# Two DiT layers on one core: the gate's modulation columns move into the down-projection, and VectorE takes half of the transpose copies

## The chip, the cores and the metric

The kernel runs on one core of one Trainium2 chip. The metric is the device time of one execution in microseconds; lower is better. Three executions of the kernel before were timed.

## The reference, cut to what matters

Two layers run over 640 tokens of width 1024: 128 context tokens and 512 latent tokens. Each layer computes

```python
sh1, sc1, ga1, sh2, sc2, ga2 = split(silu(cond) @ ada_w + ada_b, 6)   # 6 x 1024 values, for 2 conditions
h = rmsnorm(x, g_pre_mix) * (1 + sc1) + sh1
mixed = mixer(h @ w_in)              # 8 retention heads, 8 neighbourhood-attention heads
x = x + ga1 * rmsnorm(mixed @ w_out, g_post_mix)
h = rmsnorm(x, g_pre_ffn) * (1 + sc2) + sh2
x = x + ga2 * rmsnorm(conv_ffn(h, w_up, conv_w, conv_b, w_down), g_post_ffn)
```

The two conditions are one vector for the context tokens and one for the latent tokens. `ga2`, the gate of the feed-forward part, is not needed before the end of `w_down`'s product. Inside the neighbourhood attention a softmax over 320 to 384 keys is followed by a product with the values.

## The kernel before, in words

Everything is written out by hand: five engine programs (SP issues transfers, ACT, DVE, PE, POOL), each a fixed order of instructions, tied by counting semaphores. Every matmul in fp32 is made of three products of a high and a low part, so each operand is split: ACT copies the high part (`w_hi`, `m_hi`, `aT_hi`), DVE subtracts it to get the low part (`w_lo`, `m_lo`, `aT_lo`).

**The stream.** All weights come through one ring of four slots, `raw`, 128 x 1024 values (512 KB) each. `SP` loads the items of a layer in one fixed order (L541 to L548), item s into slot s % 4, and waits with each until the item four places ahead in that slot has been freed. A weight item is freed by its `split_lo` on DVE (L1350). A *column item* (128 of the 6144 modulation values, against all 1024 inputs) is not used by PE at all: DVE multiplies and sums it against each of the two conditions, `ada_first` (L1360) and `ada_second` (L1368), into `mod`; the second one frees the slot. The order of the items is `ORDER` (L97) up to the output projection (w is a weight, a is a column), then the up-projection, then `stream_down` and `stream_ada`.

**The columns.** 48 per layer. 0 to 15 (`sh1`, `sc1`) are computed one layer ahead, in the down-projection; 16 to 23 are `ga1`, 24 to 39 `sh2` and `sc2`, 40 to 47 `ga2`. Before, 19 of the columns 16 to 47 are done in the input projection and retention, 8 in the attention loop, 5 in the second half of the output projection. `times_gain` (L1378) then multiplies in a norm weight, and ACT stores a finished gate to DRAM (`store_gates`) and loads it again broadcast to all partitions (`gb_mix`, `gb_ffn`). `mod_done` counts the finished groups.

**The attention loop** runs over 20 pairs of a head group and a block of queries, in a software pipeline of NPU + 3 = 23 rounds. In round i PE computes the scores of pair i (L2369, L2371), the transposes of pair i - 1 (L2380, two heads e = 0 and 1, banks 4 and 5) and the product with the values of pair i - 2 (L2393). DVE adds the bias and takes the maximum (`na_weigh`, L1600), ACT does the exponentials (L1158) and copies the transposes of both heads from PSUM to `pt` (L1166). Every fourth round there is also the division by the sums (L1889, L1891, L2404, L1895). In round 1 to 5 DVE also has `mix_low` (L1582) and in round 5 `split_lo(31)`; in rounds 5 to 20 it has one half of a column each (L1365 or L1371).

**The down-projection** has 24 granules (two halves of 12). A granule is one weight item with one or two blocks of 128 rows of `w_down`, against the matching blocks `kt` of the activations `m`: 30 matmuls, or 15 where there is one block (granules 10, 11, 12 and 13). In its iteration `gi` ACT runs `split_hi` of weight gi + 2 and then `down_high` for the blocks of granule gi; DVE runs one column (where there is one), `split_lo` of weight gi + 2, and then `down_low` for the blocks of granule gi. The blocks 4 and 5 (granule 2) are the exception on DVE: their `down_low` stands ahead of the loop, while their `down_high` is in ACT's iteration 2, behind `split_hi` of weight 4. The first items of a half are, before: w0 w1 w2 w3 a w4 a w5 a w6 and so on, that is, weight 4 is the sixth item and lies in slot 1, and weight 5 is the eighth, in slot 3.

Of the kernel before, what the change touches and what calls it, by code (L numbers as in the profile page):

```python
# [64 lines left out]
ADA_MIX = 5 * KD  # L65
# [22 lines left out]
S_UP0 = G_IN + G_OUT + ADA - ADA_FIRST  # L88
S_DOWN0 = S_UP0 + G_UP
S_HALF = (G_DOWN + ADA_FIRST) // 2  # L90
# [9 lines left out]
assert len(W_POS) == G_IN + G_OUT and len(A_POS) == ADA - ADA_FIRST  # L100
# [12 lines left out]
def stream_down(q):  # L113

    n, i = divmod(q, G_HALF)
    return S_DOWN0 + S_HALF * n + (i if i < 4 else 2 * i - 3)


def stream_ada(col):

    if col < ADA_FIRST:
        n, i = divmod(col, ADA_FIRST // 2)
        return S_DOWN0 + S_HALF * n + 4 + 2 * i
    return A_POS[col - ADA_FIRST]
# [43 lines left out]
def build(nc, t):  # L168
    with ExitStack() as ctx:
# [154 lines left out]
        mod_done = counted("mod_done", 5, 0, 6)  # L324
# [50 lines left out]
        na_p = counted("na_p", 2 * NPU)  # L375
# [4 lines left out]
        gates_out = counted("gates_out", 16 * 4)  # L380
# [213 lines left out]
        MOD_PRE, MOD_ALL = 2, 5  # L594
# [170 lines left out]
        def _(act):  # L765
# [29 lines left out]
            def modulate(w, tt, layer):  # L795
# [4 lines left out]
                if tt == 0:  # L800
                    act.wait_ge(mod_done, at(mod_done, layer, MOD_ALL if w else MOD_PRE))
                    if w:
                        act.wait_ge(pad_done, at(pad_done, layer, 1))
# [112 lines left out]
            def store_gates(w, layer):  # L916

                for c in range(2):
                    act.dma_start(gates[layer, w, c].rearrange("(k p) -> p k", p=P),
                                  mod[:, (3 * w + 2) * KD:(3 * w + 3) * KD, c],  # L920
                                  allow_slow_non_contiguous=True).then_inc(gates_out, 16)

            def load_gates(w, gb, layer):

                act.wait_ge(gates_out, at(gates_out, layer, 32 * (w + 1)))
                act.dma_start(gb[:].rearrange("p c d -> p (c d)"),
                              gates[layer:layer + 1, w].rearrange("o c d -> o (c d)").to_broadcast([P, 2 * D])
                              ).then_inc(gates_in, 16)

# [160 lines left out]
            for layer in range(DEPTH):  # L1090
# [77 lines left out]
                for i in range(NPU + 3):  # L1168
                    for e in range(2):
                        if i < NPU:  # L1170
                            exponentials(i, e)
                        if 1 <= i < NPU + 1:
                            copy_transposed(i - 1, e)
# [6 lines left out]
                    if i == 18:  # L1180
                        act.wait_ge(mod_done, at(mod_done, layer, MOD_ALL - 1))
                        store_gates(0, layer)
# [11 lines left out]
                load_gates(0, gb_mix, layer)  # L1194
# [11 lines left out]
                def load_ffn_gates(n):  # L1206
                    for c in range(2):
# [141 lines left out]
        def _(dve):  # L1349
# [10 lines left out]
            def ada_first(col, layer):  # L1360
                s = stream_ada(col)
                dve.wait_ge(*full(s, layer))
                n = col - ADA_FIRST if col >= ADA_FIRST else col + ADA - ADA_FIRST
                dve.wait_ge(ada_part, at(ada_part, layer, n))
                dve.tensor_tensor_reduce((ada_junk if col < ADA_FIRST else ada_sq)[:], raw[:, s % 4, :], cond[:, 0, :], 1.0, ada_start(col, layer), ALU.mult,  # L1365
# [12 lines left out]
            def times_gain(f0, c0, plus, layer):  # L1378
# [1413 lines left out]
```

## Time and profile before

| | |
|---|---|
| runs | 1604.45, 1601.09, 1603.74 us; median 1603.74 us |
| span of the profiled execution | 1601.0 us |
| PE busy | 1575.8 us (98%) |
| DVE busy | 1275.6 us (80%) |
| ACT busy | 794.1 us (50%) |
| chain that ended last | PE 84%, DVE 7%, issue 2%, ACT 2%, DMA 1% |

The span runs from the first to the last instruction; a time of its own for the profiled execution is not given beside it, and the span lies 2.7 us under the median of the runs. "Busy" of PE is modelled from pipelined matmuls, so 98% is not peak speed. An idle time in brackets behind an instruction names what it waited for last.

### The profile page before, as it was taken

Reading aid. Unit: us, or ns where it says so; the run is one execution under the profiler, and the core shown is the slowest. Engines: PE = TensorE matmul, PEld = TensorE weight load, DVE = VectorE, ACT = ScalarE, POOL = GpSimd, SP = SyncE. Lnnn points to the kernel's source line nnn. Section 1 sums busy time; section 2 is a strip of 40 time slices with the busy share of each in tenths; the row PEclk is TensorE's granted clock in tenths of the full one; section 3 lists DMA queues with packets and bytes.
Section 4 is the critical chain, followed back from the end, with each engine's and each line's share of the span. In section 5 each row is a group of like instructions: output and inputs, shape, how many; then the busy total and the mean of one; then the engine's idle time right before and its main releaser. Section 6 shows DMA issues by size and latency. Waiting matters only on the chain.

```text
span 1601.0 us, 28310 instructions
## 1 busy us (share of the span) xinstructions
PE 1575.8 (98%) x9688; PEld 1389.2 (87%) x9688; DVE 1275.6 (80%) x2255; ACT 794.1 (50%) x1483; POOL 379.2 (24%) x302
## 2 busy tenths in 40 slices
PE   8999999999999999999999999999999999999998
PEld 6788898689999999888878889967899999998886
DVE  7876677968999999966669556987689999998575
ACT  5433235638655565533383323274766565563333
POOL 0031033001455455200000400700035455541000
PEclk9999999999999999999999999999999999999999
DMA  9343265361222222454414414736312222335451
GB/s 369 122 132 111 74 222 179 95 168 55 66 81 89 79 92 79 148 168 158 152 40 145 138 54 134 260 107 146 79 64 82 80 91 79 92 92 178 125 184 66
DMA packets 65494, 195.04 MB, mean 122 GB/s; under 512 B 15361, under 2 KB 16769, under 8 KB 65153
## 3 DMA queue, kind: packets, MB, share of 16 engines
q1 hardware_dynamic: 50114, 175.54, 35.1%
q10 hardware_dynamic: 15296, 18.39, 3.5%
q8 instruction: 53, 0.87, 0.3%
q14 instruction: 31, 0.25, 0.1%
HBM read 187.05 MB, written 6.85 MB: 121 GB/s over the span
## 4 chain that ended last, share of the span: by engine, by line
PE 84%; DVE 7%; issue 2%; ACT 2%; DMA 1%; ACTq 1%; DVEq 0%; SPq 0%
PE bank L2087 14%; PE bank L2088 13%; PE bank L2089 13%; PE bank L2597 10%; PE bank L2599 10%; PE bank L2598 10%; DMA raw<-in_stream 1%; PE bank L2393 1%; PE bank L2457 1%; PE bank L2455 1%; PE bank L2453 1%; PE bank L2380 1%; PE bank L2109 1%; DVE w_lo L1354 1%; PE bank L2277 1%
## 5 line engine op out<-in xcount | busy, mean ns | idle before, releaser
L778 ACT ACTIVATE w_hi<-raw 128x1024 fp32r<-128x1024 f32 (+1 forms) x120 | 123.1, 1029 | 389.0 <-PE bank L2089 325.1
L1354 DVE TENSOR_TENSOR w_lo<-raw,w_hi 128x1024 fp32r<-128x1024 f32 (+1 forms) x128 | 156.3, 1228 | 162.4 <-ACT w_hi L778 162.2
L2087 PE MATMUL bank<-w_hi,aT_lo 128*128 128x512 f32 x520 | 210.5, 405 | 2.1 <-DVE aT_lo L1787 2.0
L2088 PE MATMUL bank<-w_lo,aT_hi 128*128 128x512 f32 x520 | 206.0, 396 | 0.0
L2089 PE MATMUL bank<-w_hi,aT_hi 128*128 128x512 f32 x520 | 205.6, 395 | 0.0
L2597 PE MATMUL bank<-aT_hi,w_lo 128*128 128x322 f32 x640 | 199.8, 312 | 4.5 <-DVE u L1953 4.5
L2598 PE MATMUL bank<-aT_lo,w_hi 128*128 128x322 f32 x640 | 199.4, 312 | 0.0
L2599 PE MATMUL bank<-aT_hi,w_hi 128*128 128x322 f32 x640 | 198.6, 310 | 0.0
L1252 ACT ACTIVATE w_hi<-raw 128x512 fp32r<-128x512 f32 x200 | 117.8, 627 | 105.8 <-POOL raw L660 105.8
L2087 PE MATMUL bank<-w_hi,m_lo 128*128 128x512 f32 x400 | 158.5, 396 | 0.0
L2088 PE MATMUL bank<-w_lo,m_hi 128*128 128x512 f32 x400 | 157.3, 393 | 0.0
L2089 PE MATMUL bank<-w_hi,m_hi 128*128 128x512 f32 x400 | 157.2, 393 | 0.0
L1942 DVE TENSOR_TENSOR w_lo<-raw,w_hi 128x512 fp32r<-128x512 f32 x200 | 140.7, 734 | 0.0
L2597 PEld LDWEIGHTS bank<-aT_hi,w_lo 128*128 128x128 f32 x640 | 120.7, 189 | 6.0 <-DVE u L1953 5.0
L2598 PEld LDWEIGHTS bank<-aT_lo,w_hi 128*128 128x128 f32 x640 | 121.3, 190 | 0.0
L2599 PEld LDWEIGHTS bank<-aT_hi,w_hi 128*128 128x128 f32 x640 | 121.3, 190 | 0.0
L2087 PEld LDWEIGHTS bank<-w_hi,aT_lo 128*128 128x128 f32 x520 | 98.2, 189 | 26.5 <-DVE aT_lo L1787 3.4
L2089 PEld LDWEIGHTS bank<-w_hi,aT_hi 128*128 128x128 f32 x520 | 98.4, 189 | 23.3
L2088 PEld LDWEIGHTS bank<-w_lo,aT_hi 128*128 128x128 f32 x520 | 98.4, 189 | 20.8
L649 POOL TENSOR_TENSOR raw<-raw 128x512 f32<-128x512 f32 x40 | 52.6, 1316 | 258.6 <-DVE bank L1983 137.4
L639 POOL TENSOR_TENSOR bias<-bias,masks 128x192 f32<-128x192 f32 (+1 forms) x48 | 59.1, 1269 | 198.0 <-DMA bias<-in_bias 198.0
L2599 PE MATMUL bank<-s_hi,w_hi 128*128 128x322 f32 x320 | 99.8, 312 | 0.0
(287 smaller groups left out, 3865.9 us busy)
## 6 DMA issues: line engine op xcount, KB each, us to landing
raw<-in_stream SPq DMA_DIRECT2D x304, 512.0 KB, 3.6
lead<-in_lead SPq DMA_DIRECT2D x16, 512.0 KB, 10.6
bias<-in_bias ACTq DMA_DIRECT2D x8, 896.0 KB, 10.3
na_v<-vn ACTq DMA_DIRECT2D x2, 1280.0 KB, 5.6
x<-in_xs SPq DMA_DIRECT2D x4, 512.0 KB, 12.4
vt<-na_v ACTq DMA_DIRECT2D x16, 128.0 KB
gb_mix<-gates ACTq DMA_DIRECT2D x2, 1024.0 KB, 6.2
gb_ffn<-gates ACTq DMA_DIRECT2D x8, 256.0 KB, 4.5
```

Of the source, the lines that this page charges most:

```text
L639: i_ = pool.tensor_tensor(part, part, masks[:, m0 * CG:(m0 + n) * CG].rearrange("p (g c) -> p g c", c=CG).unsqueeze(2) .to_broadcast([P, n ...
L649: pool.tensor_tensor(g_, g_, a_, ALU.subtract).then_inc(t1_done, 1)
L778: act.activation(w_hi[:, g % 4, 0:n], raw[:, s % 4, 0:n], ACT.Copy).then_inc(hi_done, 1)
L1252: act.activation(block_of(w_hi, n), block_source(n, e), ACT.Copy).then_inc(blk_hi, 1)
L1354: dve.tensor_tensor(w_lo[:, g % 4, 0:n], raw[:, s % 4, 0:n], w_hi[:, g % 4, 0:n].bitcast(F32), ALU.subtract).then_inc(raw_free[s % 4], 1)
L1942: i_ = dve.tensor_tensor(block_of(w_lo, n), block_source(n, e), block_of(w_hi, n).bitcast(F32), ALU.subtract)
L2087: pe.matmul(out, ll, rh, start=start, stop=False)
L2088: pe.matmul(out, lh, rl, start=False, stop=False)
L2089: return pe.matmul(out, lh, rh, start=False, stop=stop)
L2597: pe.matmul(out, wl, rhs_hi[:, k, :], start=k == 0, stop=False)
L2598: pe.matmul(out, wh, rhs_lo[:, k, :], start=False, stop=False)
L2599: i_ = pe.matmul(out, wh, rhs_hi[:, k, :], start=False, stop=k == HP - 1)
```

## The change

1. Columns 40 to 47 (`ga2`) leave the attention's place in the stream; the eight a's between w31 and w32 are gone from `ORDER`. DVE's attention loop has no column any more (columns 35 to 39 now fill the five places in the output projection).
2. They go to the down-projection of the same layer, four in each half, ahead of the next layer's eight of that half. So a half has 12 columns in place of 8. They are spread over the iterations i = 4 to 11 of a half as 2, 1, 2, 1, 2, 1, 2, 1. The items of a half are now w0 w1 w2 w3 a a w4 a w5 a a w6 a w7 and so on: weight 4 is the seventh item (slot 2), weight 5 the ninth (slot 0).
3. DVE copies the transposes of the second head (e = 1), ACT only those of the first. PE waits on a semaphore of each.
4. The gate's store is split in two and moves from the output projection into ACT's iterations gi = 7 and 19 (before `down_high`), the loads to gi = 9 and 21; before they stood ahead of the loop (just before `down_weight(3)`) and at gi = 14.
5. `times_gain` for `sh2`/`sc2` and `ga2` are moved with their columns, so `mod_done` counts 6.

```diff
-ORDER = ("wwww" "wwww" "waawaaww" "wwaawwaa" "wwww" "wwawawaaa" "wwaawaawwaawww" "aaaaaaaa" "waawaawaw")
+ORDER = ("wwww" "wwww" "waawaaww" "wwaawwaa" "wwww" "wwawawaaa" "wwaawaawwaawww" "waawaawaw")
...
 def stream_down(q):
     n, i = divmod(q, G_HALF)
-    return S_DOWN0 + S_HALF * n + (i if i < 4 else 2 * i - 3)
+    return S_DOWN0 + S_HALF * n + (i if i < 4 else i + down_columns(i + 1))
+
+def down_columns(i):
+    return 0 if i < 4 else (3 * (i - 4) + 1) // 2
...
                 for i in range(NPU + 3):
-                    for e in range(2):
-                        if i < NPU:
-                            exponentials(i, e)
-                        if 1 <= i < NPU + 1:
-                            copy_transposed(i - 1, e)
+                    if i < NPU:
+                        exponentials(i, 0)
+                    if 1 <= i < NPU + 1:
+                        copy_transposed(i - 1, 0)
+                    if i < NPU:
+                        exponentials(i, 1)
...
-                act.wait_ge(mod_done, at(mod_done, layer, MOD_ALL))
-                store_gates(1, layer)
                 turn_ffn(layer)
-                act.wait_ge(gates_out, at(gates_out, layer, 64))
...
-                load_ffn_gates(0)
                 down_weight(3)
...
-                    if gi == G_HALF + 2:
-                        act.wait_ge(y_copied, at(y_copied, layer, 2 * NT))
-                        load_ffn_gates(1)
+                    if i == 7:
+                        store_ffn_gates(n, layer)
+                    if i == 9:
+                        if n:
+                            act.wait_ge(y_copied, at(y_copied, layer, 2 * NT))
+                        load_ffn_gates(n)
...
+            def copy_transposed(u, layer):
+                n = P * len(spans_of(PAIRS[u]))
+                dve.wait_ge(na_t, at(na_t, layer, 2 * u + 2))
+                if u >= 2:
+                    dve.wait_ge(na_av, at(na_av, layer, u - 1))
+                dve.tensor_copy(pt[:, u % 2, 1, 0:n], bank[NA_T[1]][:, 0:n]).then_inc(na_q, 1)
...
-                    if 5 <= i < 21:
-                        (ada_first if i % 2 else ada_second)(ADA_FIRST + 19 + (i - 5) // 2, layer)
+                    if 1 <= i < NPU + 1:
+                        copy_transposed(i - 1, layer)
...
                         n, i = divmod(gi + 2, G_HALF)
-                        if i >= 4:
-                            ada(ADA_FIRST // 2 * n + i - 4, layer)
+                        for col in ADA_DOWN[n][down_columns(i):down_columns(i + 1)]:
+                            ada(col, layer)
+                        if i == 7:
+                            dve.wait_ge(*freed(stream_ada(ADA_DOWN[n][HALF_K - 1]), layer))
+                            times_gain(ADA_LATE + HALF_K * n, C_PF + HALF_K * n, 0.0, layer, HALF_K).then_inc(mod_done, 1)
                         split_lo(W_DOWN0 + gi + 2, layer)
```

What the instructions look like in order, at three places. First DVE at the start of the down-projection, from the `down_low` of blocks 4 and 5 to that of blocks 6 and 7, before (L1365 and L1371 are the two parts of a column, L1354 is `split_lo`, L1987 `down_low`; the `ISA mod` rows read out a sum):

```order
L1987 TENSOR_TENSOR m_lo<-m,m_hi 128x642 x2
L1365 ISA ada_junk,mod<-raw,cond 128x1024
L1365 ISA mod 128x1
L1371 ISA raw,mod<-raw,cond 128x1024
L1371 ISA mod 128x1
L1354 TENSOR_TENSOR w_lo<-raw,w_hi 128x1024
L1365 ISA ada_junk,mod<-raw,cond 128x1024
```

and the same place in the changed kernel (L2008, L1380, L1386 and L1370 are the same lines there):

```order
L2008 TENSOR_TENSOR m_lo<-m,m_hi 128x642 x2
L1380 ISA ada_junk,mod<-raw,cond,par 128x1024
L1380 ISA mod 128x1
L1386 ISA raw,mod<-raw,cond,par 128x1024
L1386 ISA mod 128x1
L1380 ISA ada_junk,mod<-raw,cond,par 128x1024
L1380 ISA mod 128x1
L1386 ISA raw,mod<-raw,cond,par 128x1024
L1386 ISA mod 128x1
L1370 TENSOR_TENSOR w_lo<-raw,w_hi 128x1024
```

A second column stands ahead of `split_lo` of weight 4; the columns are now those of the gate, which start from `par`. Second, ACT at the same place, before: `down_weight(3)`, the SiLU, then `split_hi` of weight 4 and `down_high` of blocks 4 and 5.

```order
L1229 ACTIVATE cvg<-bank,par 128x322
L1230 ACTIVATE cvg<-bank,par 128x320
L1208 DMA gb_ffn<-gates 128x512 x2
L1267 ACTIVATE w_hi<-raw 128x1024
L1213 ACTIVATE cvg<-cvg 128x642
L778 ACTIVATE w_hi<-raw 128x1024
L1261 ACTIVATE m_hi<-m 128x642 x2
```

and now:

```order
L1243 ACTIVATE cvg<-bank,par 128x322
L1244 ACTIVATE cvg<-bank,par 128x320
L1281 ACTIVATE w_hi<-raw 128x1024
L1227 ACTIVATE cvg<-cvg 128x642
L788 ACTIVATE w_hi<-raw 128x1024
L1275 ACTIVATE m_hi<-m 128x642 x2
```

Only the two loads of `gb_ffn` have gone from here; `m_hi` still stands behind the split of weight 4. Third, DVE in the attention's rounds 5 and 6, before:

```order
L1354 TENSOR_TENSOR w_lo<-raw,w_hi 128x1024
L1365 ISA ada_sq,mod<-raw,cond,par 128x1024
L1365 ISA mod 128x1
L1889 RECIPROCAL rec<-esum 128x8
L1891 COPY nao<-bank 128x512
L1600 ISA sp,nmax<-bank,bias 128x384
L1600 ISA nmax 128x1
L1371 ISA raw,mod<-raw,cond,par 128x1024
L1371 ISA mod 128x1
L1895 TENSOR_TENSOR nao<-nao,bank 128x512
```

and now:

```order
L1370 TENSOR_TENSOR w_lo<-raw,w_hi 128x1024
L1623 COPY pt<-bank 128x384
L1910 RECIPROCAL rec<-esum 128x8
L1912 COPY nao<-bank 128x512
L1615 ISA sp,nmax<-bank,bias 128x384
L1615 ISA nmax 128x1
L1623 COPY pt<-bank 128x384
L1916 TENSOR_TENSOR nao<-nao,bank 128x512
```

In each round a half column has given way to a copy of 128 x 384.

## Rows read from the trace of the kernel before

**Rows 1.** Page, part 4: the chain that ended last, by engine.
```profile
PE 84%; DVE 7%; issue 2%; ACT 2%; DMA 1%; ACTq 1%; DVEq 0%; SPq 0%
```
**Rows 2.** By stretch: length; PE, PEld, DVE, ACT, POOL busy; clock, DMA share, GB/s.
```profile
262.00:284.00 22.00, 19.74 (x192) 13.77 (x191) 14.19 (x38) 17.48 (x48) 0.00 (x0) 1.00 0.30 98
284.00:320.00 36.00, 35.25 (x357) 25.03 (x357) 34.38 (x91) 26.23 (x87) 0.00 (x0) 1.00 0.36 91
665.00:680.00 15.00, 15.00 (x66) 11.95 (x65) 15.00 (x19) 5.06 (x7) 4.33 (x1) 1.00 0.55 175
```
**Rows 3.** Timeline of the attention, rounds 6 to 20: start us, us, instruction, [idle before <-releaser].
```profile
282.10 1.09 PE L2404 MATMUL bank<-ident,rec 128*64 128x128 f32 x16 [0.41 <-DVE nao L1891]
282.91 1.28 DVE L1371 CUSTOM_DVE_ANT_0 raw<-raw,cond,par 128x1024 f32<-128x1024 f32 x1
284.72 0.48 DVE L1600 CUSTOM_DVE_ANT_0 sp<-bank,bias 128x320 f32<-128x320 f32 x1
284.75 0.52 PE L2380 MATMUL bank<-ident,sp 128*128 128x128 f32 x3 [0.33 <-ACT pt L1166]
...
286.76 1.21 PE L2380 MATMUL bank<-ident,sp 128*128 128x128 f32 x6
...
295.61 0.87 PE L2380 MATMUL bank<-ident,sp 128*128 128x128 f32 x6
...
319.04 0.45 ACT L1166 ACTIVATE pt<-bank 128x128 f32<-128x128 f32 x2 [1.55 <-PE bank L2380]
```
**Rows 4.** Groups by line and form, ACT and DVE: busy us, mean ns.
```profile
L1166 ACT ACTIVATE pt<-bank 128x384 f32<-128x384 f32 x64 | 30.3, 474 | 0.0
L1891 DVE COPY nao<-bank 128x512 f32<-128x512 f32 x10 | 6.5, 649 | 1.4 <-PE bank L2393 1.4
```
**Rows 5.** Timeline of DVE at the start of the down-projection; last row: layer 1.
```profile
668.31 2.94 DVE L1987 TENSOR_TENSOR m_lo<-m,m_hi 128x642 fp32r<-128x642 f32 x2
671.16 1.22 DVE L1365 CUSTOM_DVE_ANT_0 ada_junk<-raw,cond 128x1024 f32<-128x1024 f32 x1
...
673.45 1.22 DVE L1354 TENSOR_TENSOR w_lo<-raw,w_hi 128x1024 fp32r<-128x1024 f32 x1
...
678.02 1.55 DVE L1987 TENSOR_TENSOR m_lo<-m,m_hi 128x642 fp32r<-128x642 f32 x2
...
1450.04 2.94 DVE L1987 TENSOR_TENSOR m_lo<-m,m_hi 128x642 fp32r<-128x642 f32 x2
```
**Rows 6.** Timeline of ACT and of SP's issues at the same place.
```profile
659.04 0.33 SPq L548 DMA_DIRECT2D raw<-in_stream  x1
666.49 1.06 ACT L778 ACTIVATE w_hi<-raw 128x1024 fp32r<-128x1024 f32 x1 [1.07 <-PE bank L2089]
667.41 0.33 SPq L548 DMA_DIRECT2D raw<-in_stream  x1
667.46 1.35 ACT L1261 ACTIVATE m_hi<-m 128x642 fp32r<-128x642 f32 x2
668.54 0.33 SPq L548 DMA_DIRECT2D raw<-in_stream  x1
673.63 1.06 ACT L778 ACTIVATE w_hi<-raw 128x1024 fp32r<-128x1024 f32 x1 [4.82 <-PE bank L2089]
680.58 1.06 ACT L778 ACTIVATE w_hi<-raw 128x1024 fp32r<-128x1024 f32 x1 [4.62 <-PE bank L2089]
```
**Rows 7.** Transfers: issue to landing, `raw` in 655 to 700 us; the gates' stores.
```profile
DMA to landing us min/median/max: 3.4/3.6/4.6
...
gates<-mod ACTq DMA_DIRECT2D x4, 4.0 KB, 11.1
```
**Rows 8.** Timeline of ACT and DVE at the start of the second half.
```profile
739.59 1.22 DVE L1365 CUSTOM_DVE_ANT_0 ada_junk<-raw,cond 128x1024 f32<-128x1024 f32 x1
...
747.19 1.56 DVE L1987 TENSOR_TENSOR m_lo<-m,m_hi 128x642 fp32r<-128x642 f32 x2
...
750.22 1.06 ACT L778 ACTIVATE w_hi<-raw 128x1024 fp32r<-128x1024 f32 x1 [2.95 <-PE bank L2089]
```

More of the change, by code:

```diff
@@ L115, in stream_down @@
     n, i = divmod(q, G_HALF)
-    return S_DOWN0 + S_HALF * n + (i if i < 4 else 2 * i - 3)
+    return S_DOWN0 + S_HALF * n + (i if i < 4 else i + down_columns(i + 1))
+def down_columns(i):
+    return 0 if i < 4 else (3 * (i - 4) + 1) // 2
 def stream_ada(col):
-    if col < ADA_FIRST:
-        n, i = divmod(col, ADA_FIRST // 2)
-        return S_DOWN0 + S_HALF * n + 4 + 2 * i
+    for n in range(2):
+        if col in ADA_DOWN[n]:
+            a = ADA_DOWN[n].index(col)
+            return S_DOWN0 + S_HALF * n + a + next(i for i in range(4, G_HALF) if down_columns(i + 1) > a)
     return A_POS[col - ADA_FIRST]
@@ L800, in modulate @@
                 if tt == 0:
-                    act.wait_ge(mod_done, at(mod_done, layer, MOD_ALL if w else MOD_PRE))
+                    act.wait_ge(mod_done, at(mod_done, layer, MOD_FFN if w else MOD_PRE))
                     if w:
@@ L1362, in ada_first @@
                 dve.wait_ge(*full(s, layer))
-                n = col - ADA_FIRST if col >= ADA_FIRST else col + ADA - ADA_FIRST
-                dve.wait_ge(ada_part, at(ada_part, layer, n))
-                dve.tensor_tensor_reduce((ada_junk if col < ADA_FIRST else ada_sq)[:], raw[:, s % 4, :], cond[:, 0, :], 1.0, ada_start(col, layer), ALU.mult,
+                dve.wait_ge(ada_part, at(ada_part, layer, ADA_ORDER.index(col)))
+                dve.tensor_tensor_reduce((ada_sq if ADA_FIRST <= col < ADA_LATE else ada_junk)[:], raw[:, s % 4, :], cond[:, 0, :], 1.0, ada_start(col, layer), ALU.mult,
                                          ALU.add, mod[:, col, 0:1]).then_inc(ada_part, 1)
@@ L1376, in ada, with times_gain @@
                 ada_second(col, layer)
-            def times_gain(f0, c0, plus, layer):
+            def times_gain(f0, c0, plus, layer, n=KD):
                 c0 += layer * NPAR
-                return dve.scalar_tensor_tensor(mod[:, f0:f0 + KD, :], mod[:, f0:f0 + KD, :], plus,
-                                                par[:, c0:c0 + KD].unsqueeze(2).to_broadcast([P, KD, 2]),
+                return dve.scalar_tensor_tensor(mod[:, f0:f0 + n, :], mod[:, f0:f0 + n, :], plus,
+                                                par[:, c0:c0 + n].unsqueeze(2).to_broadcast([P, n, 2]),
                                                 ALU.add, ALU.mult)
@@ L1392, in modulate @@
                 dve.wait_ge(norm_tp, at(norm_tp, layer, i + 1))
-                dve.wait_ge(mod_done, at(mod_done, layer, MOD_ALL if w else MOD_PRE))
+                dve.wait_ge(mod_done, at(mod_done, layer, MOD_FFN if w else MOD_PRE))
                 for k in range(KV):
@@ L1879, in _ @@
                         split_lo(31, layer)
-                    if 5 <= i < 21:
-                        (ada_first if i % 2 else ada_second)(ADA_FIRST + 19 + (i - 5) // 2, layer)
+                    if 1 <= i < NPU + 1:
+                        copy_transposed(i - 1, layer)
                     if i == 14:
-                        dve.wait_ge(*freed(stream_ada(ADA_MIX - 1), layer))
-                        times_gain(4 * KD, C_GF, 1.0, layer).then_inc(mod_done, 1)
+                        dve.wait_ge(*freed(stream_ada(3 * KD - 1), layer))
                         times_gain(2 * KD, C_PM, 0.0, layer).then_inc(mod_done, 1)
@@ L1910, in _ @@
                     split_lo(W_OUT0 + 4 + g, layer)
-                    for col in range(ADA_MIX + 3 + 2 * g, ADA_MIX + 3 + 2 * g + n):
+                    for col in range(ADA_FIRST + 19 + 2 * g, ADA_FIRST + 19 + 2 * g + n):
                         ada(col, layer)
-                dve.wait_ge(*freed(stream_ada(ADA - 1), layer))
-                times_gain(5 * KD, C_PF, 0.0, layer).then_inc(mod_done, 1)
+                dve.wait_ge(*freed(stream_ada(ADA_LATE - 1), layer))
+                times_gain(4 * KD, C_GF, 1.0, layer).then_inc(mod_done, 1)
                 split_lo(W_OUT0 + 7, layer)
@@ L2377, in na_transposes @@
                     if u >= 1:
-                        pe.wait_ge(na_p, at(na_p, layer, 2 * u - 1 + e))
+                        copied = na_q if e else na_p
+                        pe.wait_ge(copied, at(copied, layer, u))
                     for i, (c0, p0, n, tile) in enumerate(spans_of(PAIRS[u])):
@@ L2384, in na_values @@
                 g, jb = PAIRS[u]
-                pe.wait_ge(na_p, at(na_p, layer, 2 * u + 2))
+                pe.wait_ge(na_p, at(na_p, layer, u + 1))
+                pe.wait_ge(na_q, at(na_q, layer, u + 1))
                 if jb == 0 and g >= 2:
```

46 lines of the change are left out of this document (27 added, 19 removed).

## The prediction, made before the changed kernel was run

> **What bounds the kernel.** I read the page's chain of waits first. PE carries 84% of it and DVE only 7% [rows 1], so an instruction taken from DVE or ACT is worth something only at the few places where PE stands behind them, and one added costs nothing until PE has to wait for it. So I read the two stretches that the change touches. In the attention loop PE is busy for 19.74 of 22 us and 35.25 of 36 us [rows 2]: it idles for 2.26 + 0.75 = 3.0 us per layer, most of it in the first third. That is all that lighter ACT and DVE programs can win there, 6 us in both layers. At the start of the down-projection PE is busy for all of 15 us, and so is DVE [rows 2]: there is no slack to be seen on DVE just where the change adds work. The prediction is decided there.
>
> **Attention: what the change saves.** It removes 16 half columns per layer from DVE (1.28 us in [rows 3]) and adds 20 copies of 128 x 384 out of PSUM. The trace has no such copy on DVE: a copy of 128 x 512 takes 649 ns there, and one of 128 x 384 takes 474 ns on ACT [rows 4]. Three quarters of the first are 0.49 us, and some of an instruction doesn't shrink with its size, so I take 0.52 us; the ends change nothing on PE. ACT loses 20 copies of 0.47 us [rows 4]. DVE is 16 x 1.28 - 20 x 0.52 = 10 us lighter per layer, but only PE's waits count.
> - Rounds 6 and 7. The half column at 282.91 holds the weighing back to 284.72, although its scores are there earlier; PE's transposes then idle for 0.33 us, and the next six take 1.21 us where six without a wait take 0.87 [rows 3]. Without the columns the weighing starts 0.8 us earlier, behind the division only. I take back the 0.33 and 0.34 us and 0.2 us that the loading of the weights hides: 0.9 us.
> - The last rounds. Both copies of pair 19 wait for PE's transposes and run one behind the other on ACT (0.45 us together), with PE behind them [rows 3]; in parallel they take half: 0.25 us. Small waits of PE elsewhere: 0.15 us.
> - No gain in rounds 2 to 4, where PE waits for `mix_low`, which keeps its place. No gain at PE's 0.41 us before 282.10 [rows 3] either: the copy of pair 4 now stands behind `mix_low` and `split_lo(31)` on DVE and comes about 0.5 us later than ACT's did. The second head's transposes start that much later and use up what the earlier copy of `nao` gives.
>
> Sum: 0.9 + 0.25 + 0.15 = 1.3 us per layer. It can't be more than 3.0 [rows 2]; if the late copy in round 5 is not absorbed, it is a loss of 0.5 with nothing against it.
>
> **Output projection and its turn: nothing.** DVE has five columns there as before and one `times_gain` either way. ACT loses two store issues that stood behind finished work; PE is never idle there, and it covers this.
>
> **Down-projection: the added work.** DVE takes 2.29 us for a column (671.16 to 673.45, [rows 5]), 1.14 us for a `split_lo`, and 1.48 us for two `down_low`. Two iterations cost 3 x 2.29 + 2 x 2.62 = 12.1 us, against two granules of PE of 6.95 us each (673.63 to 680.58, [rows 6]) = 13.9 us. So in the steady part DVE keeps up. At the start it doesn't.
>
> *Weight 4 comes late.* Before, it goes to slot 1 and is issued at 659.04. Now the two columns go first, and it gets slot 2, whose issue is the one at 667.41 [rows 6], when DVE has done `split_lo` of weight 2. A load lands after 3.6 us [rows 7]: 671.0. ACT splits it from 671.1 (now 666.49) and only then makes `m_hi` of blocks 4 and 5, from 672.05 to 673.4 (now from 667.46). DVE has their `down_low` ahead of everything else, so it stands idle from 668.3 with two columns ready in `raw`, and ends at 674.3 in place of 671.16 [rows 5]. PE wants these blocks when granule 1 ends, at 673.5 [rows 6]: it starts at 674.4, **0.9 us** late.
>
> *Then two columns stand in front.* DVE: 674.3 + 4.58 (two columns) + 1.14 + 2.29 + 1.14 + 1.48 = 684.95 for blocks 6 and 7, which now are ready at 679.5, 1.0 us before granule 3 [rows 5, 6]. PE wants them at 674.4 + 6.95 = 681.35: **3.7 us** late, with 0.1 us of signalling. Weight 5 (slot 0, freed by the first column at 676.6) lands at 680.4 and its split and the blocks' `m_hi` are done by 682.8: hidden.
>
> *Granule 4*: 684.95 + 4.58 + 1.14 + 1.48 = 692.15, wanted at 685.05 + 6.95 = 692.0: **0.2 us** with the signal. Then DVE gains 1.8 us in every two granules, and nothing is late.
>
> *Second half.* Granules 12 and 13 take half the time, so DVE has to catch up again: from 739.59 [rows 8] it needs 4.58 + 1.14 + 2.29 + 1.14 + 1.48 = 10.65, until 750.25; now it is done with blocks 0 and 1 at 748.7. Granule 14 ends at about 750.1 [rows 8]: **0.2 us**, and the next double column costs **0.2 us** more (757.45 against 757.3).
>
> Sum: 0.9 + 3.7 + 0.2 + 0.4 = 5.2 us per layer. Layer 1 has the same schedule 781.7 us later [rows 5]: 10.4 us. A load that takes 3.4 or 4.6 us [rows 7] changes the first term by -0.2 or +1.0 per layer. The other bound is that DVE starts unhindered by weight 4, with the double columns alone; that is the second rival.
>
> The Trainium skill ("DMA: Bandwidth & Descriptors", section on the anatomy of one DMA) gives about 2.0 us plus the bytes over 436 GB/s, which is 3.2 us for such a load, fitted on loads that GpSimd issues. By that estimate weight 4 would be 0.4 us earlier than by the row, and the sum 0.8 us lower; I go by the row, since it is of this very load at this place.
>
> **The gate's transfers.** A store takes 11.1 us to land [rows 7]. ACT now waits for it two granules (13.9 us) after its issue: 2.8 us of room, so nothing. The four issues stand before `down_high` in iterations where ACT is idle for over 4 us per granule (4.62 us in [rows 6]). The loads at gi = 9 and 21 have two granules before they are used. The two loads that leave ACT at the start lay beside idle time.
>
> **Sum against the runs.** 10.4 - 2.6 = +7.8 us. The sum is made on an execution with a span of 1601.0 us, 2.7 us below the runs' median; it is a difference, and I add it to the median: 1603.7 + 7.8 = **1611.5 us**. A measurement of this kernel can tell about 0.2% (3.2 us) from no change.
>
> **The rivals.**
> - *Slower as worked out* (DVE is late at the start of the down-projection, and weight 4's slot is why): 1611.5 us, between 1606.5 (gain of 2.5 and stalls of 4 us per layer) and 1616. Chance 0.66.
> - *No change: only the second column counts.* If weight 4's place in the ring costs nothing, blocks 6 and 7 are ready at 679.5 + 2.29 = 681.8, wanted at 680.5: 1.4 us, with the second half's 0.4 us 1.8 per layer. 3.6 - 2.6 = +1.0: 1604.7 us. For it: the columns' transfers themselves come early. Against it: ACT is a fixed order, and `m_hi` of blocks 4 and 5 stands behind the split of weight 4. Chance 0.12.
> - *Faster: the attention decides.* All of PE's 3.0 us per layer come back, since both engines it waits for are lighter, and the stalls stay under that. With the 1.8 us of the last rival: 3.6 - 6.0 = -2.4; with none -6.0, 1597.7 us. The point is a stall of 1.3 us per layer by my gain, 3.0 by the largest. For it: DVE is busy for 34.38 of 36 us there [rows 2]. Against it: most of PE's idle time is in the early rounds, at `mix_low`, which stays. Chance 0.07.
> - *Slower by more: DVE doesn't recover.* The ring's items now free each other in a closer sequence (weight 6 waits for the column of iteration 3, weight 7 for a column of iteration 4), and small stores go on beside it. With loads of 4.6 us, or 1 us lost at every second granule, 4 to 8 us are added: 1616 to 1620 us. Against it: DVE's 1.8 us per two granules. Chance 0.15.
>
> **Range and chances.** 1611.5 is the likeliest. The range goes from 1604.5, which takes in the second case, to 1617.5, the lower part of the last. Slower by over 0.2%: 0.66 + 0.15 = 0.81. Within 0.2%: 0.12. Faster: 0.07.
>
> **What would show it.** In the changed profile the attention should be some 1.3 us shorter, with no column in it and PE's second wait of 0.33 us gone. The SP issue after 667 should be weight 4's; ACT's first split in the loop should wait for a transfer and begin near 671 less the attention's gain; DVE should idle for some 4 us before the `down_low` of blocks 4 and 5. PE should show waits for `m_lo` of about 0.9 and 3.7 us in the first three granules of each layer, and two small ones in the second half. The prediction is wrong if ACT's `m_hi` of blocks 4 and 5 is on time, if PE has no idle time at the start of the down-projection, or if PE waits at every second granule.

## The result and the profile after

| | before | changed |
|---|---|---|
| median of the runs | 1603.64 us (4 runs, 1601.09 to 1604.45) | 1629.55 us (4 runs, 1627.23 to 1630.42) |
| span of the profiled execution | 1601.0 us | 1625.4 us |
| attention, from PE's first transposes to its last, either layer | 55.23 us | 53.43 us |
| down-projection, start of granule 0 to the last matmul that reads the low part of `m`, layers 0 and 1 | 153.59 and 152.66 us | 169.39 and 166.16 us |

The changed kernel is slower: ratio 1.0162, 95% interval 1.0150 to 1.0174. I had forecast 1611.5 us and a range up to 1617.5. The sign was right and the size was not: +25.9 us in place of +7.8. In the two stretches of the table it gains 3.6 us and loses 29.3 us; the difference is 25.7 us. The two spans differ by 24.4 us only, because the profiled execution of the kernel before has one stretch at half clock in the up-projection of layer 1, for 1.4 us, which the changed one doesn't have (last section).

The page of the changed kernel, parts 1 and 4 (rows that answer to [rows 1]):

```profile
PE 1582.1 (97%) x9688; PEld 1392.6 (86%) x9688; DVE 1290.9 (79%) x2297; ACT 782.4 (48%) x1443; POOL 378.2 (23%) x302
...
PE 74%; DVE 12%; issue 4%; DMA 3%; ACT 2%; ACTq 1%; DVEq 0%; SPq 0%
```

PE's share of the chain falls by ten points; DVE, the issues and DMA take them. That DMA is among them is the first sign of something the prediction had not costed. The waits of PE, changed kernel; columns: us in total, times, longest:

```profile
PE bank L2111 <- DVE m_lo L2008: 18.2, 8, 4.4
```

This row has no counterpart before: 18.2 us of new waits, all for `down_low` (waits under 0.15 us are not in it). Where they lie shows in the starts of the granules (the first matmul of each in PE's timeline; a granule takes 6.95 us when nothing is late):

| layer 0 | before | changed | longer by |
|---|---|---|---|
| granules 0 to 3 | 659.30 to 687.29 | 656.62 to 692.09 | 7.48 us |
| 4 to 13 | to 742.98 | to 747.89 | 0.11 us |
| 14 to 16 | to 763.88 | to 770.13 | 1.34 us |
| 17, 18 | to 777.80 | to 784.05 | 0.00 us |
| 19 to 21 | to 798.66 | to 811.78 | 6.87 us |

In layer 1 the same groups are 7.56, 0.04, 1.31, 0.00 and 4.60 us longer. So there are three places per layer; the first two were forecast, the third was not. First the start. ACT, changed kernel (answers to [rows 6]):

```profile
668.28 1.06 ACT L788 ACTIVATE w_hi<-raw 128x1024 fp32r<-128x1024 f32 x1 [5.55 <-DMA raw<-in_stream]
669.25 1.35 ACT L1275 ACTIVATE m_hi<-m 128x642 fp32r<-128x642 f32 x2
677.73 1.06 ACT L788 ACTIVATE w_hi<-raw 128x1024 fp32r<-128x1024 f32 x1 [7.13 <-DMA raw<-in_stream]
```

DVE, changed kernel (answers to [rows 5]):

```profile
670.07 1.56 DVE L2008 TENSOR_TENSOR m_lo<-m,m_hi 128x642 fp32r<-128x642 f32 x2 [4.38 <-ACT m_hi L1275]
...
681.06 1.56 DVE L2008 TENSOR_TENSOR m_lo<-m,m_hi 128x642 fp32r<-128x642 f32 x2
```

That is the mechanism as forecast: the split of weight 4 waits for its transfer, `m_hi` stands behind it, DVE idles for 4.38 us, and then two columns stand in front of blocks 6 and 7, and the one of weight 5. These are columns of the gate, which start from `par`: DVE takes 2.41 us for each (671.56 to 673.97), where the sum had 2.29. PE's first matmul of granule 3:

```profile
682.77 0.76 PE L2111 MATMUL bank<-w_hi,m_lo 128*128 128x512 f32 x1 [3.80 <-DVE m_lo L2008]
```

Granule 3 itself then takes 9.32 us in place of 6.95. The stretches around it and around granule 20; columns as in [rows 2], the clock third from the end:

```profile
679.00:682.00 3.00, 0.00 (x0) 0.00 (x0) 3.00 (x5) 1.04 (x2) 0.00 (x0) 0.82 0.78 300
682.00:685.00 3.00, 2.23 (x5) 1.82 (x6) 3.00 (x6) 0.00 (x0) 0.00 (x0) 0.50 0.75 251
685.00:688.00 3.00, 3.00 (x9) 2.34 (x8) 3.00 (x7) 2.31 (x3) 0.00 (x0) 0.54 0.61 187
688.00:691.00 3.00, 3.00 (x15) 2.42 (x14) 3.00 (x6) 0.00 (x0) 0.00 (x0) 1.00 0.86 238
...
795.00:800.00 5.00, 4.46 (x11) 3.52 (x12) 5.00 (x8) 2.35 (x3) 0.00 (x0) 0.50 0.96 370
```

The same stretch of the kernel before, for comparison:

```profile
685.00:688.00 3.00, 3.00 (x15) 2.41 (x14) 1.76 (x4) 0.45 (x1) 0.00 (x0) 1.00 0.54 190
```

PE is idle for all of 679 to 682, and behind it the granted clock stands at 0.50, the 1.2 GHz level, where the kernel before has 1.00: 9 matmuls in 3 us in place of 15. This second price of a wait was in no term of the prediction.

The third place. ACT, changed kernel, around the gate's second store:

```profile
777.36 0.98 ACTq L929 DMA_DIRECT2D gates<-mod  x2
778.44 1.37 ACT L1275 ACTIVATE m_hi<-m 128x642 fp32r<-128x642 f32 x2
791.61 1.06 ACT L788 ACTIVATE w_hi<-raw 128x1024 fp32r<-128x1024 f32 x1 [11.80 <-DMA raw<-in_stream]
```

The transfers of 774 to 800 us, changed kernel (count, KB each, median us to landing):

```profile
raw<-in_stream SPq DMA_DIRECT2D x8, 512.0 KB, 9.0
...
gates<-mod ACTq DMA_DIRECT2D x2, 2.0 KB, 14.2
```

Beside the store the median load of the stream takes 9.0 us, against 3.6 in [rows 7], and 12.6 us in the same place of layer 1 (1568 to 1592 us). I had asked only when the store itself would land. The trace of the kernel before would have told the rest. Its transfers of 346 to 361 us, around the store in the output projection:

```profile
raw<-in_stream SPq DMA_DIRECT2D x1, 512.0 KB, 12.8
gates<-mod ACTq DMA_DIRECT2D x2, 4.0 KB, 12.3
```

There nobody was waiting for that load; in the down-projection somebody is.

### The profile page after: what moved, and what is told of

Read it like the earlier page. It is cut to its first block, busy times and chain, and to the rows that moved or that the text cites. A ratio compares the mean times of both kernels' runs of the same rounds, so it can differ in the third digit from the quotient of the medians.

```text
span 1625.4 us, 28346 instructions
## 1 busy us (share of the span) xinstructions
PE 1582.1 (97%) x9688; PEld 1392.6 (86%) x9688; DVE 1290.9 (79%) x2297; ACT 782.4 (48%) x1443; POOL 378.2 (23%) x302
## 4 chain that ended last, share of the span: by engine, by line
PE 74%; DVE 12%; issue 4%; DMA 3%; ACT 2%; ACTq 1%; DVEq 0%; SPq 0%
PE bank L2111 11%; PE bank L2112 10%; PE bank L2113 10%; PE bank L2623 9%; PE bank L2625 9%; PE bank L2624 9%; DMA raw<-in_stream 3%; DVE ada_junk L1380 2%; PE bank L2419 2%; DVE w_lo L1370 2%; DVE m_lo L2008 1%; PE bank L2405 1%; PE bank L2483 1%; PE bank L2481 1%; PE bank L2479 1%
## 5 line engine op out<-in xcount | busy, mean ns | idle before, releaser
L1370 DVE TENSOR_TENSOR w_lo<-raw,w_hi 128x1024 fp32r<-128x1024 f32 (+1 forms) x128 | 156.5, 1230 | 141.5 <-ACT w_hi L788 141.2
L2111 PE MATMUL bank<-w_hi,m_lo 128*128 128x512 f32 x400 | 162.8, 407 | 18.5 <-DVE m_lo L2008 18.2
L2112 PE MATMUL bank<-w_lo,m_hi 128*128 128x512 f32 x400 | 160.8, 402 | 0.0
L2111 PEld LDWEIGHTS bank<-w_hi,m_lo 128*128 128x128 f32 x400 | 77.3, 193 | 41.0 <-issue 23.3
```

The source lines that it names most:

```text
L1370: dve.tensor_tensor(w_lo[:, g % 4, 0:n], raw[:, s % 4, 0:n], w_hi[:, g % 4, 0:n].bitcast(F32), ALU.subtract).then_inc(raw_free[s % 4], 1)
L2111: pe.matmul(out, ll, rh, start=start, stop=False)
L2112: pe.matmul(out, lh, rl, start=False, stop=False)
```

## The experiments

Ten kernels, each beside runs of the kernel before on the same chip (medians 1603.19 to 1603.55 us). Two theories were left after the profile: that the early columns and the store are two separate causes (A in most expectations), and rivals that put all on one of them or on something else. "Changed" means the changed kernel.

### a_late: the columns later

```diff
 def down_columns(i):
-    return 0 if i < 4 else (3 * (i - 4) + 1) // 2
+    return 0 if i < 4 else i - 4 if i < 8 else 4 + 2 * (i - 8)
```

> Changed kernel, but the 12 columns of a half are spread as 1, 1, 1, 1, 2, 2, 2, 2 over the iterations 4 to 11 in place of 2, 1, 2, 1, 2, 1, 2, 1, so the first items of a half stand in the ring as in the kernel before. Theory A (the start of each half is what the double column costs): no wait before granules 2, 3 and 15, no halved clock in granule 3; saves 7.5 + 1.2 us per layer, 17 us in all: about 1612 us, if the last four iterations (4.58 + 2.62 = 7.2 us of DVE against 6.95 of PE) stay hidden. Theory B (what counts is the ring's pace beside the gate's store, which now falls among the double columns): the wait before granule 20 or 21 grows to 7 us or more and a wait shows behind the store of the first half too: 1617 to 1623 us.

Measured: 1624.30 us, ratio 1.0125 [1.0108, 1.0142], above the numbers of both theories. Each had half of it. Granules 2, 3 and 15 show no wait and keep the kernel before's pace (granule 4 starts 27.98 us after granule 0, before 27.99). But waits stand behind the stores now: 3.77 and 4.50 us in layer 0, 6.63 and 4.62 us in layer 1, before granules 8 and 20. ACT's splits behind the store of gi = 7, layer 0:

```profile
714.98 0.63 ACT L788 ACTIVATE w_hi<-raw 128x512 fp32r<-128x512 f32 x1 [12.15 <-DMA raw<-in_stream]
715.51 1.35 ACT L1275 ACTIVATE m_hi<-m 128x642 fp32r<-128x642 f32 x2
718.77 0.63 ACT L788 ACTIVATE w_hi<-raw 128x512 fp32r<-128x512 f32 x1 [1.91 <-DMA raw<-in_stream]
```

In the changed kernel the store of gi = 7 had cost PE nothing. With two columns per granule beside it, it does. That fits a price that depends on how many items the ring must bring while the store lasts. It isn't the whole of it: in the changed kernel the stores of gi = 7 and 19 have the same three columns per two granules beside them. The loads beside the first took up to 11.2 us and PE waited for none; beside the second they took up to 16.3 us and PE waited. Why the second is the slower is not settled.

### a_nostore: without the gate's stores

```diff
-                store_gates(1, HALF_K * n, HALF_K * (n + 1), layer)
```

(and the loads of `gb_ffn` read the mixer's gate, with no wait on the stores)

> Changed kernel without the four stores of the feed-forward gate per layer (left out: the feed-forward gate's values; the loads of the gate bring the mixer's gate instead, so the output is another). Theory A (the small pieces of the stores slow the loads of the stream): loads of the stream at 774 to 800 us take some 3.6 to 4.6 us again, the waits of 4.39 and 2.98 us before granule 20 and the clock that they cost go; saves 6.9 and about 5 us: 1618 us. Theory B (DVE's 12 columns or, in layer 0, the loads of the next layer's inputs do it): the wait of layer 0 stays over 2 us, and the time above 1624 us.

Measured: 1616.68 us, ratio 1.0082 [1.0065, 1.0099]: theory A's number within 1.4 us. This kernel leaves the feed-forward gate's values out. Granules 17 to 23 keep their pace in both layers. The waits at the start stay as they were (1.07 and 3.78 us in layer 0). In 774 to 800 us, where the next layer's loads run in layer 0:

```profile
raw<-in_stream SPq DMA_DIRECT2D x7, 512.0 KB, 5.4
```

So those loads alone bring the median to 5.4 us, without a wait of PE; the store brings it to 9.0. In layer 1, where no next layer is loaded, the median without the store is 3.6 us, with it 12.6.

### b_stores: the stores moved in the kernel before

```diff
-                store_gates(1, layer)
                 turn_ffn(layer)
...
-                    if gi == G_HALF + 2:
-                        act.wait_ge(y_copied, at(y_copied, layer, 2 * NT))
-                        load_ffn_gates(1)
+                    if i == 7:
+                        store_gates(1, KD // 2 * n, KD // 2 * (n + 1), layer)
+                    if i == 9:
+                        if n:
+                            act.wait_ge(y_copied, at(y_copied, layer, 2 * NT))
+                        load_ffn_gates(n)
```

> Kernel before, with the feed-forward gate's store cut in two and moved to gi = 7 and 19 and the loads to gi = 9 and 21, as the change does; the columns stay. Theory A (the stores cost only because the ring has 2.5 items per granule in place of 2): loads of the stream beside the stores take 7 to 10 us here as well, but PE waits less than 1 us for them: 1603 to 1606 us. Theory B (the stores stall the stream by themselves): a wait of over 2 us before granule 20 or 21 and a halved clock, 1610 us or more.

Measured: 1603.28 us, ratio 1.0003 [0.9994, 1.0013], and no wait for `m_lo` in the down-projection. Yet its transfers of 774 to 800 us are slow too:

```profile
raw<-in_stream SPq DMA_DIRECT2D x6, 512.0 KB, 7.8
```

The same stores at the same place cost nothing with 2 items per granule and, in the changed kernel, 11.5 us with 2.5.

### a_row6: the same store in rows

PE transposes the four finished columns of each condition (128 x 4 into 4 x 128) ahead of granules 6 and 18, ACT copies them out of PSUM, and 8 rows of 512 bytes are stored per half in place of 1024 pieces of 4 bytes.

```diff
+                        if i == 6:
+                            pe.wait_ge(mod_done, at(mod_done, layer, MOD_LATE + n))
+                            if n:
+                                pe.wait_ge(gt_cp, at(gt_cp, layer, 1))
+                            k0 = 5 * KD + HALF_K * n
+                            for c in range(2):
+                                i_ = pe.transpose(bank[7][0:HALF_K, c * P:(c + 1) * P], mod[:, k0:k0 + HALF_K, c], ident[:])
+                            i_.then_inc(gt_tp, 1)
...
-                store_gates(1, HALF_K * n, HALF_K * (n + 1), layer)
+                act.activation(ada_sq[0:HALF_K, 0:2 * P], bank[7][0:HALF_K, 0:2 * P], ACT.Copy).then_inc(gt_cp, 1)
+                act.wait_ge(gt_cp, at(gt_cp, layer, n + 1))
+                for c in range(2):
+                    act.dma_start(gates[layer, 1, c, HALF_K * n * P:HALF_K * (n + 1) * P].rearrange("(k p) -> k p", p=P),
+                                  ada_sq[0:HALF_K, c * P:(c + 1) * P]).then_inc(gates_out, 16)
```

> Changed kernel with its columns as they are (2, 1, 2, 1 and so on) and only the gate's store in rows, with PE's transposes ahead of granule 6. Theory A (the number of small pieces is what delays the loads, not the place of the store): the waits before granule 20 go as in a_nostore, those before granules 2, 3 and 15 stay: 1616 to 1618 us. Theory B (a store of any form costs): a wait of over 1 us stays before granule 20, 1621 us or more.

Measured: 1617.30 us, ratio 1.0082 [1.0067, 1.0098], the ratio of a_nostore. The same bytes leave at the same place, and the wait before granule 20 is gone; those before granules 2, 3 and 15 stay. The loads of 774 to 800 us are as without a store (5.4 us there), and those of layer 1 take 3.6 us again:

```profile
raw<-in_stream SPq DMA_DIRECT2D x8, 512.0 KB, 5.1
```

It is the small pieces, not the store, that held up the loads.

### a_w4first: weight 4 ahead of its columns

```diff
-    return S_DOWN0 + S_HALF * n + (i if i < 4 else i + down_columns(i + 1))
+    return S_DOWN0 + S_HALF * n + (i if i <= 4 else i + down_columns(i + 1))
...
+                        if i == 4:
+                            split_lo(W_DOWN0 + gi + 2, layer)
                         for col in ADA_DOWN[n][down_columns(i):down_columns(i + 1)]:
                             ada(col, layer)
```

> Changed kernel, but weight 4 of each half lies ahead of its two columns in the ring, and DVE splits it ahead of them. Theory A (weight 4's late load and the doubled column are two separate costs, and a wait of PE of some 4 us takes the clock with it): PE's wait of 0.99 us before granule 2 goes, that of 3.8 us before granule 3 falls to about 1.4 us (the price of one more column of 2.29 us against 1.0 us of room), and the 2.4 us that granule 3 lost to the halved clock come back. Saves 1.0 + 2.4 + 2.4 = 5.8 us per layer, 11.5 us in all: 1618 us. Theory B (it is the columns alone, wherever weight 4 lies): the wait before granule 3 stays above 3 us and the time within 3 us of 1629.5.

Measured: 1628.64 us, ratio 1.0151 [1.0134, 1.0168]: theory B's time, though not for its reason. The start did improve: no wait before granule 2, one of 1.91 us in place of 3.80 before granule 3. But that one halves the clock as well (granule 3 takes 8.58 us), the wait before granule 15 grows from 0.68 to 2.26 us, and that before granule 20 from 4.39 to 6.17 us. ACT and DVE at the start, and DVE in the second half:

```profile
676.00 1.06 ACT L788 ACTIVATE w_hi<-raw 128x1024 fp32r<-128x1024 f32 x1 [7.62 <-DMA raw<-in_stream]
676.96 1.35 ACT L1275 ACTIVATE m_hi<-m 128x642 fp32r<-128x642 f32 x2
...
679.10 1.21 DVE L1370 TENSOR_TENSOR w_lo<-raw,w_hi 128x1024 fp32r<-128x1024 f32 x1
680.24 1.55 DVE L2008 TENSOR_TENSOR m_lo<-m,m_hi 128x642 fp32r<-128x642 f32 x2
...
744.49 1.23 DVE L1370 TENSOR_TENSOR w_lo<-raw,w_hi 128x1024 fp32r<-128x1024 f32 x1 [1.50 <-ACT w_hi L788]
```

ACT waits for the transfer of weight 5, but that is not what holds PE: its split ends at 677.0 and DVE, busy without a gap from 664 to 691 us, takes it up at 679.10. What is left of the wait is work of DVE: three columns of 2.41 us in a row in place of two of 2.29, 2.65 us more, against 0.8 us of room (679.5 to 680.3 in the kernel before). That is more than the 1.4 us expected, and enough to halve the clock. In the second half DVE now has to wait 1.50 us for ACT's split of weight 4 before it can begin the two columns, where the changed kernel began them at once: so the wait before granule 15 grows. The start gains 3.8 us per layer (granules 0 to 3), the second half loses 1.6 and 1.3 us, and granules 19 to 21 lose 1.6 and 3.8 us. The last needn't be the edit's: in a_actcopy (below), with the order of the changed kernel, the waits before granule 20 are 5.69 and 3.62 us in place of 4.39 and 2.98.

### b_wait4 and b_wait8: what a wait of PE costs

The kernel before, with four or eight dummy subtractions on DVE ahead of the `down_low` of blocks 6 and 7.

```diff
+                        if gi == 3 and kt == 6:
+                            for j in range(4):
+                                if j:
+                                    dve.wait_ge(delay, at(delay, layer, j))
+                                dve.tensor_tensor(bank[7][:], cond[:, 0, 0:W], cond[:, 1, 0:W], ALU.subtract).then_inc(delay, 1)
```

> Kernel before, with four dummy subtractions of 128 x 512 values (about 0.68 us each, 2.7 us) on DVE ahead of the down_low of blocks 6 and 7, in both layers: those blocks were ready 1.0 us before PE wanted them, so PE waits about 1.8 us before granule 3, with the ring as before. Theory A (a wait also halves the granted clock behind it): granule 3 then takes 8.6 us in place of 6.95; 2 x (1.8 + 1.65) = 6.9 us, 1610 us. Theory B (only the wait counts): 2 x 1.8 = 3.6 us, 1607 us, and the granule takes 6.95 us.

Measured: 1609.66 us, ratio 1.0043 [1.0026, 1.0060]. PE waits 2.05 and 2.12 us, and granule 3 takes 8.60 and 8.59 us.

> The same with eight dummy subtractions (5.4 us): PE waits about 4.5 us before granule 3. Theory A (the clock falls for a stretch that depends little on the wait's length): granule 3 takes 8.6 to 9.3 us; 2 x (4.5 + 1.7 to 2.4) = 12.4 to 13.8 us, about 1616 us. Theory B (only the wait counts): 9 us, 1612 us. A third way, that the clock's loss grows with the wait: granule 3 over 10 us, 1619 us or more.

Measured: 1617.24 us, ratio 1.0084 [1.0067, 1.0101]. PE waits 4.99 and 4.98 us, and granule 3 takes 9.31 and 8.90 us: 2.0 to 2.4 us for the clock. A wait 2.4 times as long costs little more of clock, so the third way (a loss that grows with the wait) falls. No column was added here and no store moved: the clock's loss comes with the wait itself. Two stretches of b_wait8, layer 0:

```profile
683.00:686.00 3.00, 0.00 (x0) 0.00 (x0) 2.93 (x6) 0.54 (x1) 0.00 (x0) 0.71 0.00 0
686.00:689.00 3.00, 2.89 (x7) 2.34 (x8) 3.00 (x5) 0.00 (x0) 0.00 (x0) 0.50 0.00 0
```

### a_actcopy: both copies on ACT again

```diff
                     if i < NPU:
                         exponentials(i, 1)
+                    if 1 <= i < NPU + 1:
+                        copy_transposed(i - 1, 1)
...
-                    if 1 <= i < NPU + 1:
-                        copy_transposed(i - 1, layer)
```

(the first pair of lines is ACT's, the second DVE's)

> Changed kernel with both heads' transposes copied by ACT again, the columns staying in the down-projection. The attention from PE's first transposes to its last took 55.23 us in the kernel before and 53.43 in the changed one, in both layers. Theory A (most of the 1.8 us is DVE's freedom from the columns): 53.6 to 54.2 us, the whole within 2 us of 1629.5. Theory B (it is the copies running on two engines): 54.8 us or more, the whole 3 us slower than the changed kernel, 1632 us.

Measured: 1628.57 us, ratio 1.0163 [1.0146, 1.0180] as for the changed kernel; the attention takes 53.36 and 53.35 us. All of the 1.8 us came from taking the columns away. Two engines copying gave nothing.

### c_row and c_row6: both costs mended

c_row is a_late's columns with the store in rows, where PE makes its transposes ahead of granule 7 (19).

> Changed kernel with two edits: the columns spread as 1, 1, 1, 1, 2, 2, 2, 2 (as in a_late), and the gate stored in rows: PE transposes the four finished columns of either condition, ACT copies the 4 x 256 values out of PSUM and stores 8 rows of 512 bytes per half in place of 1024 pieces of 4 bytes. Theory A (the small pieces are what delays the loads, and the double column at the start was the other cost): in a_late PE's granules 7, 8, 19 and 20 of both layers were 28.1 us longer in sum than their 6.95 us; all of it goes, and PE's transposes add some 0.4 us: 1624.3 - 28.1 + 0.4 = about 1596.6 us, 0.4% faster than the kernel before. Theory B (any store and load of the gate beside a ring with 2.5 items per granule delays it, or two columns in each of four granules, 7.2 us of DVE against 6.95, do): waits of over 2 us stay before granules 8 or 20, 1603 us or more.

Measured: 1622.62 us, ratio 1.0121 [1.0104, 1.0139], with waits of 3.64, 3.65, 3.64 and 3.64 us before granules 7 and 19. Waits as equal as these point to a fixed order rather than to transfers. ACT shows it:

```profile
708.69 0.37 ACT L947 ACTIVATE ada_sq<-bank 4x256 f32<-4x256 f32 x1 [6.04 <-PE bank L2701]
709.10 0.62 ACTq L950 DMA_DIRECT2D gates<-ada_sq  x2
709.82 1.37 ACT L1283 ACTIVATE m_hi<-m 128x642 fp32r<-128x642 f32 x2 [0.75 <-ACT ada_sq L947]
```

This was my own fault: ACT's iteration 7 runs while PE works on granule 6. It waited for transposes that stood behind granule 6, with granule 7's `m_hi` queued behind that wait. c_row6 makes them ahead of granule 6 (`i == 6`, as in a_row6).

> As c_row, but PE makes the transposes of the gate ahead of granule 6 (18) in place of 7 (19). In c_row ACT waited 6.04 us for them in its iteration 7, and down_high of that granule stood behind it, so PE waited 3.64 us four times for its own transposes. Theory A (that order was the only fault of c_row): the four waits go, with them the clock behind them: granules 7, 8, 19 and 20 of both layers were 22.1 us longer than 6.95 us each; 1622.6 - 22.1 = 1600.5 us, the down-projection from its first to its last granule as in the kernel before (153.6 and 152.7 us), the attention 1.8 us per layer shorter: faster than before by some 0.2%. Theory B (any store beside this ring delays it, or two columns per granule do): at least two waits over 1 us stay, 1603 us or more.

Measured: 1601.08 us in 11 runs against 1603.55 us in 15, ratio 0.9982 [0.9973, 0.9991]: the changed kernel with both costs mended is 0.18% faster than the kernel before, and 28 us faster than the change as made. The chain, page of c_row6, part 4:

```profile
PE 86%; DVE 6%; issue 2%; DMA 1%; ACT 1%; ACTq 1%; DVEq 0%; SPq 0%
```

There is no wait for `m_lo` in the down-projection. From granule 0 to its last matmul it takes 154.03 and 153.12 us, 0.45 us over the kernel before: granules 5 and 6 (17 and 18) together take 0.2 us more with PE's small transposes, twice the 0.1 I had expected for each place. The attention takes 53.43 and, in layer 1 of the profiled execution, 54.52 us. There PE waits once for 1.7 us for ACT's exponential, and the clock behind it is at 0.57 in 1046 to 1050 us. ACT was held by two transfers of the stream, the second of them directly ahead of the exponential:

```profile
1039.83 1.06 ACT L790 ACTIVATE w_hi<-raw 128x1024 fp32r<-128x1024 f32 x1 [6.46 <-DMA raw<-in_stream]
1042.64 1.06 ACT L790 ACTIVATE w_hi<-raw 128x1024 fp32r<-128x1024 f32 x1 [1.03 <-DMA raw<-in_stream]
```

Why these came late in this execution stays open.

## Why the prediction was right and wrong

**The sign was right, and so was the mechanism at the start of both halves:** weight 4's late load, then the doubled column. The size was wrong, by two terms that the sum didn't have. The steps against what was measured, per layer:

| step | predicted | measured |
|---|---|---|
| attention | -1.3 us | -1.80 us |
| wait before granule 2 | 0.9 us | 0.99 and 0.94 us |
| wait before granule 3 | 3.7 us | 3.80 and 3.78 us |
| granule 4 | 0.2 us | no wait |
| clock behind granule 3's wait | no term | 2.37 us in either layer |
| second half, granules 14 to 16 | 0.4 us | 1.34 and 1.31 us, of it waits of 0.68 and 0.69 (granule 15), 0.13 and 0.11 (granule 16) |
| the gate's store | "so nothing" | 6.87 and 4.60 us |

**The attention** gained more than I took, within my bound of 3.0. The step "in parallel they take half: 0.25 us" was wrong: a_actcopy has all of the gain without it. The DVE copy came out at 552 ns, for 520 taken; that changed nothing. I had also kept PE's 0.41 us before 282.10 [rows 3] as lost. In the changed kernel PE's named waits for transposes and `nao` are down from 1.2 us to 0.4 in 262 to 320 us of layer 0; the other 1.0 us has no wait with a name; I take it to lie inside groups such as the six transposes of 1.21 us [rows 3], of which I had counted one. The waits of 262 to 320 us, changed kernel:

```profile
PE bank L2419 <- DVE aT_lo L1597: 1.0, 1, 1.0
PE bank L2405 <- DVE pt L1623: 0.4, 1, 0.4
```

**The step that failed first** is "A store takes 11.1 us to land ... 2.8 us of room, so nothing". It priced the store's own landing and not what the store does to the loads beside it. Runs a_nostore, a_row6 and b_stores show the term: 11.5 us in both layers together, from small pieces, nothing with 2 items of the ring per granule, and with 2.5 only at the second store of a layer. The rival "slower by more" named the right ingredients ("small stores go on beside it") but priced loads at 4.6 us, where their medians were 9.0 and 12.6, and expected DVE's 1.8 us per two granules to absorb it.

**The second step that failed** is the conversion of a wait into time at one for one ("Sum: 0.9 + 3.7 + 0.2 + 0.4 = 5.2 us per layer"). Behind 3.80 us of wait came 2.37 us of half clock, behind 4.39 us 2.34 us, behind 2.98 us 1.43 us: 8.5 us in all, of which 3.8 are also in the store's 11.5. b_wait4 and b_wait8 show this in the kernel before, with nothing else changed.

Together: start 15.0, second half 2.7, store 11.5 and 0.2 elsewhere make 29.3 us, less 3.6. The waits at the places I had named sum to 5.6 and 5.5 us against 5.2 predicted per layer, so that part of the sum held. The two sizes that it had slightly wrong are the column (2.41 us with `par`, not 2.29) and the end of granule 14 (749.96 in the kernel before, not 750.1). The clock at the start (4.7 us) and the store (11.5 us) are 16.2 of the 18.1 us by which the forecast was short; the second half, 1.9 us over its 0.8 in both layers, is most of the rest. In the trace of before I had the store's neighbour (12.8 us) within reach and did not look at it.

The estimate that I had worked out from the Trainium skill ("DMA: Bandwidth & Descriptors", section on the anatomy of one DMA), 3.2 us for such a load, has a fixed part and one that grows with the bytes, and nothing for what else is in flight. Here the load took 3.6 us [rows 7], and beside 4-byte pieces 9.0 and 12.6 us in the median; the measurement decides.

## What to carry to other kernels

When a transfer is moved, price what it does to its neighbours before its own landing: look up, in the trace you have, how long the loads beside that very store take. A transposed store of a few KB in 4-byte pieces is cheap only where nobody waits for a load; a transpose on PE and a few 512-byte rows made it harmless here for 0.2 us. And a wait of PE of 2 us or more is to be priced with a slow stretch behind it that may or may not come (nothing to 2.7 us here), so work that is added to a filled engine goes where its lead has built up, not at the start of a stage.

## What the runs showed of the hardware

- The granted clock behind a wait of PE is not settled by the wait's length. Ahead of each wait below the clock stood at 1.00. In b_wait4 2.05 us cost 1.65 us, in b_wait8 4.99 us cost 2.4. But in c_row, layer 0, a wait of 3.64 us cost 0.16 us and the clock stayed at 1.00, while in layer 1 the same wait at the same granule cost 2.66 us. The two, layer 0 first:

```profile
712.00:715.00 3.00, 2.70 (x12) 2.21 (x13) 3.00 (x6) 0.96 (x2) 0.00 (x0) 1.00 0.00 0
...
1500.00:1503.00 3.00, 2.74 (x7) 2.19 (x8) 3.00 (x6) 0.92 (x2) 0.00 (x0) 0.50 0.01 3
```

  The clearest case is a wait that every kernel here has once per layer, of 2.2 to 2.3 us, in the up-projection (L2597 in the kernel before). In the 12 profiled executions, two layers each, the clock fell to 0.50 behind it in 11 cases and stayed at 1.00 in 13. From that wait to the down-projection it is 229.0 to 229.1 us where the clock fell and 227.6 where it didn't: 1.4 to 1.5 us for the clock alone. The kernel before has one of each, layer 0 first:

```profile
431.00:434.00 3.00, 2.30 (x15) 2.30 (x16) 2.90 (x7) 1.29 (x3) 2.58 (x2) 1.00 0.61 175
...
1211.00:1214.00 3.00, 2.00 (x7) 2.00 (x8) 2.90 (x7) 0.99 (x2) 2.30 (x2) 0.63 0.51 175
```

  Waits of 2.26 and 1.97 us (a_w4first, before granule 15) and of 3.62 us (a_actcopy, layer 1, before granule 20) left it at 1.00 as well, and so did all those of 0.7 to 1.2 us (changed kernel, a_nostore, a_row6). What decides stays open.
- Two stores of 2 KB in 4-byte pieces on ACT's queue bring the median 512 KB load on SP's queue from 3.6 us to 7.8 (b_stores), 9.0 and 12.6 us (changed kernel) in stretches of some 25 us, single loads to 16.3 us; the same bytes in 512-byte rows don't show as a wait of PE anywhere. The Trainium skill ("DMA: Bandwidth & Descriptors", section on queues, rings and completion order, under arbitration) says that each DMA engine takes turns between the queues it has work for, a packet at a time, which fits loads that advance only between pieces of a store. No run here shows the turns themselves.
